# Gate and up of the second layer as seven block products on one Trainium2 core

## The reference, cut to what matters

```python
FF_DIM = 2816
def swiglu(h, w_gu, w_dn):
    g, u = jnp.split(h @ w_gu, 2, axis=-1)
    return (jax.nn.silu(g) * u) @ w_dn
x = post_norm(x, g2 * swiglu(modulate(x, sh2, sc2), w_gate_up[layer], w_down[layer]), ln2_w[layer], ln2_b[layer])
```

## Time and profile before

| what | us |
|---|---|
| median of 3 runs | 1629.88 |
| lowest and highest run | 1629.54, 1630.83 |
| profiled execution, first to last instruction | 1629.1 |
| TensorE busy | 1592.0 |
| VectorE busy | 783.9 |
| ScalarE busy | 427.1 |
| POOL busy | 855.8 |

### The profile page before, as it was taken

How to read it: one execution, slowest core, us unless ns; L and a number is a source line. 1 busy time by engine, 2 the same in 40 slices (tenths; PEclk the granted TensorE clock), 3 DMA queues, 4 the chain that set the end, 5 groups by cost and what they waited for, 6 DMA issues and landing times.

```text
span 1629.1 us, 23301 instructions
## 1 busy us (share of the span) xinstructions
PE 1592.0 (98%) x9335; PEld 1358.5 (83%) x9335; DVE 783.9 (48%) x1201; ACT 427.1 (26%) x920; POOL 855.8 (53%) x850
## 2 busy tenths in 40 slices
PE   7999999999999999999999999999999999999997
PEld 5788666778999988899999888886778888888886
DVE  4352265549663414443555396715659322520038
ACT  5512365425400011100002065216534200200011
POOL 4643044633464444544445455613485777777772
PEclk9999999999999999999999999999999999999999
DMA  9312143121453312244561121210032642233321
GB/s 343 118 52 78 41 149 118 57 78 52 119 165 92 117 40 78 67 146 124 177 210 60 66 78 53 78 52 9 15 85 74 195 142 91 90 95 101 104 91 52
DMA packets 161369, 160.89 MB, mean 99 GB/s; under 512 B 6520, under 2 KB 120296, under 8 KB 161264
## 3 DMA queue, kind: packets, MB, share of 16 engines
q1 hardware_dynamic: 140928, 121.40, 24.5%
q10 hardware_dynamic: 20336, 38.03, 7.2%
HBM read 157.31 MB, written 2.10 MB: 98 GB/s over the span
## 4 chain that ended last, share of the span: by engine, by line
PE 86%; DVE 7%; ACT 4%; issue 2%; DMA 1%; SPq 0%; DVEq 0%; POOL 0%; ACTq 0%
PE ps L843 24%; PE ps L845 24%; PE ps L844 24%; PE ps L1123 3%; PE ps L1147 2%; PE ps L1171 2%; ACT probs L1845 1%; DVE resid L2271 1%; DVE act_lo L2184 1%; DVE st L2212 1%; DVE ps L2193 1%; ACT hbuf L1647 1%; PE ps L966 1%; ACT probs_more L1845 1%; PE ps L927 1%
## 5 line engine op out<-in xcount | busy, mean ns | idle before, releaser
L757 POOL TENSOR_SCALAR ring_hi<-stage 128x512 fp32r<-128x512 f32 x352 | 245.3, 697 | 519.5 <-PE ps L845 450.0
L760 POOL TENSOR_TENSOR ring_lo<-stage,ring_hi 128x512 fp32r<-128x512 f32 x352 | 480.8, 1366 | 29.4
L843 PE MATMUL ps<-act_hi,ring_hi 128*128 128x384 f32 (+2 forms) x1088 | 379.1, 348 | 0.5 <-POOL ring_lo L760 0.5
L845 PE MATMUL ps<-act_hi,ring_lo 128*128 128x384 f32 (+2 forms) x1088 | 377.8, 347 | 0.0
L844 PE MATMUL ps<-act_lo,ring_hi 128*128 128x384 f32 (+2 forms) x1088 | 377.8, 347 | 0.0
L843 PE MATMUL ps<-ring_hi,act_hi 128*128 128x512 f32 (+1 forms) x711 | 280.6, 395 | 0.4 <-DVE act_lo L2184 0.4
L845 PE MATMUL ps<-ring_hi,act_lo 128*128 128x512 f32 (+1 forms) x711 | 273.5, 385 | 0.0
L844 PE MATMUL ps<-ring_lo,act_hi 128*128 128x512 f32 (+1 forms) x711 | 273.1, 384 | 0.0
L843 PEld LDWEIGHTS ps<-act_hi,ring_hi 128*128 128x128 f32 x1088 | 204.6, 188 | 13.9 <-POOL ring_lo L760 0.7
L845 PEld LDWEIGHTS ps<-act_hi,ring_lo 128*128 128x128 f32 x1088 | 204.5, 188 | 13.2
L844 PEld LDWEIGHTS ps<-act_lo,ring_hi 128*128 128x128 f32 x1088 | 204.6, 188 | 13.0
(11 more groups left out here) (278 smaller groups left out, 2046.1 us busy)
## 6 DMA issues: line engine op xcount, KB each, us to landing
stage<-in_w_gate_up_dram SPq DMA_DIRECT2D x88, 512.0 KB, 5.1
mod_stage<-in_w_mod_dram ACTq DMA_DIRECT2D x56, 512.0 KB, 4.2
stage<-in_w_in_dram SPq DMA_DIRECT2D x18, 1024.0 KB, 5.0
stage<-in_w_down_dram SPq DMA_DIRECT2D x16, 1024.0 KB, 5.0
stage<-in_w_mod_dram SPq DMA_DIRECT2D x12, 1024.0 KB, 5.2
start_mod<-in_w_mod_dram SPq DMA_DIRECT2D x16, 512.0 KB, 9.7
stage<-in_w_down_dram SPq DMA_DIRECT2D x8, 768.0 KB, 4.4
stage<-in_w_out_dram SPq DMA_DIRECT2D x16, 256.0 KB, 4.5
```

The lines of the kernel that those rows point to most:

```text
L757: nc.gpsimd.tensor_scalar(hi_, stage[:, par, j * 512:(j + 1) * 512], 1.0, 0.0, ALU.mult, ALU.add).then_inc(w_hi, 1)
L760: nc.gpsimd.tensor_tensor(lo_, stage[:, par, j * 512:(j + 1) * 512], hi_.bitcast(F32), ALU.subtract).then_inc(w_ready, 1)
L843: nc.tensor.matmul(o, a_hi, b_hi, start=first, stop=False)
L845: return nc.tensor.matmul(o, a_lo, b_hi, start=False, stop=last)
```

## The change

The second layer's chunks 3 to 10 of the first half and 0 to 10 of the second half are made by a seven-product scheme for 2 x 2 blocks. The blocks of the weights are gate and up (rows of the result) by the lower and upper 512 of the contraction; those of the activations are the two halves of the contraction by two halves of 256 latent tokens. Each of the seven products is 4 x 3 = 12 matmuls of 256 columns on one slot of 128 x 512.

- SyncE writes the stage as four blocks, `(g k c)` and not `(k g c)`.
- Four of the left operands are blocks of the weights (one of them changed in place by a sum), three are sums of blocks in `w_sum`. VectorE makes the four sums (`fast_sum`), ScalarE the seven high parts (`fast_highs`), POOL five low parts (`fast_low`), VectorE the low parts 3 and 4 (`fast_lows`, `BY_DVE`).
- The right operands that are sums or differences of token blocks are made once: VectorE `t_sums` (seven instructions) at the start of the first half, ScalarE `t_highs` (six), VectorE `t_lows` (six) behind chunk 0's product. For this the four tiles of modulated rows are all kept (`h_rows`).
- TensorE's `fast_chunk` puts products 0 to 3 into four banks' halves, and 4, 5, 6 on top of banks of 0, 1 and 3. ScalarE copies product 0 out (`fast_copy`); VectorE joins in five steps (`fast_half`), waiting for products 2, 3, 5 and 6.
- A chunk takes 7 slots and not 4.

The diff, cut to its core:

```diff
+FIRST_FAST = {(DEPTH - 1, 0): 3, (DEPTH - 1, 1): 0}
+STEPS = 7
+BY_DVE = (3, 4)
...
+        def fast_left(u, i):
+            block = {0: 0, 1: 2, 4: 1, 5: 3}
+            if i in block:
+                return stage[:, u % 2, block[i] * 512:(block[i] + 1) * 512]
+            return w_sum[{3: 0, 2: 1, 6: 2}[i]][:, :]
...
+            def fast_low(l, u, g, i):
+                pool.wait_ge(ring_used, g - 7)
+                pool.wait_ge(sem("fast_hi"), slots_of((ACT_HIGH, DVE_LOW), g))
+                nc.gpsimd.tensor_tensor(ring_lo[:, g % RING, :], fast_left(u, i), ring_hi[:, g % RING, :].bitcast(F32),
+                                        ALU.subtract).then_inc(w_ready, 1)
...
+                def fast_chunk(g, f):
+                    c = fast_number(l, fh, f)
+                    if f >= 2:
+                        need(pe, "hid_ready", l, f0 + f - 1)
+                    elif f == 1:
+                        need(pe, "dn_read", l, 2 * len(tiles_of(l)))
+                    for i, (gu, r) in enumerate(((0, 0), (1, 0), (1, 1), (0, 1), (0, 0), (1, 0), (0, 1))):
+                        slot_wait(pe, g + i)
+                        if c == 0 and i in T_DONE:
+                            need(pe, "t_done", l, T_DONE[i])
+                        if i == 4:
+                            need(pe, "fast_copy", l, c + 1)
+                        elif i > 4:
+                            need(pe, "fast_read", l, 3 * c + i - 3)
+                        b_hi, b_lo = fast_right(i)
+                        for k in range(4):
+                            w = slice(k * P, (k + 1) * P)
+                            mm = joined(fast_bank(l, fh, f, gu, r), ring_hi[:, (g + i) % RING, w], ring_lo[:, (g + i) % RING, w],
+                                        b_hi[:, k, :], b_lo[:, k, :], i < 4 and k == 0, k == 3)
+                        mm.then_inc(ring_used, 1)
...
+            def fast_highs(l, fh, f):
+                g, u = gu_slot(l, fh, f), UNIT0[(l, f"gu{fh}")] + f
+                c = fast_number(l, fh, f)
+                unit_wait(act, u)
+                for i in range(STEPS):
+                    act.wait_ge(ring_used, g + i - 7)
+                    if i in SUM_STEP:
+                        need(act, "fast_sum", l, 4 * c + SUM_STEP[i])
+                    a.activation(ring_hi[:, (g + i) % RING, :], fast_left(u, i), ACT.Copy).then_inc(sem("fast_hi"), 1)
+                    if i == 0 and f and is_fast(l, fh, f - 1):
+                        fast_copy(l, fh, f - 1)
...
+                if (l, fh) == (DEPTH - 1, 0):
+                    t_highs(l)
                 for f in range(HALF):
+                    if f < HALF - 1 and is_fast(l, fh, f + 1):
+                        fast_highs(l, fh, f + 1)
...
                         if fh == 0:
                             act.wait_ge(ffn_mod_used, ffn_units((l, fh)))
                         for j in range(4 if fh else 2):
                             hid_high(l, 2 * fh, j)
-                    chunk(f, g0 + 4 * f + 4, fh * HALF + f - 1 if f >= 2 else None)
+                    chunk(f, gu_slot(l, fh, f) + 4, fh * HALF + f - 1 if f >= 2 else None)
                     load_mods(f)
...
+            def fast_half(l, fh, f, between):
+                g, c = gu_slot(l, fh, f), fast_number(l, fh, f)
+                _, g2, u1, u2 = (fast_bank(l, fh, f, gu, r) for gu in range(2) for r in range(2))
+                more = f < HALF - 1
+                def after(i):
+                    dve.wait_ge(ring_used, g + i + 1)
+                if more:
+                    fast_sum(l, fh, f + 1, 0)
+                    fast_sum(l, fh, f + 1, 1)
+                after(2)
+                need(dve, "fast_copy", l, c + 1)
+                done(v.tensor_tensor(both[:, :], one[:, :], u2, ALU.add), "fast_read")
+                done(v.tensor_tensor(one[:, :], both[:, :], u1, ALU.add), "fast_read")
+                if more:
+                    fast_sum(l, fh, f + 1, 2)
+                after(3)
+                done(v.tensor_tensor(u2, one[:, :], g2, ALU.add), "fast_read")
+                if more:
+                    fast_sum(l, fh, f + 1, 3)
+                    fast_lows(l, fh, f + 1)
+                between()
+                after(5)
+                link(v.tensor_tensor(u1, both[:, :], u1, ALU.add))
+                after(6)
+                done(v.tensor_tensor(g2, both[:, :], g2, ALU.add), "fast_gate")
...
                 for f in range(HALF):
+                    if is_fast(l, fh, f):
+                        fast_half(l, fh, f, first_slices if f == HALF - 1 else lambda: ffn_terms((l, fh), f))
+                        need(dve, "silu_ready", l, fh * HALF + f + 1)
+                        chunk(f)
+                        continue
...
                     chunk(f)
+                    if (l, fh, f) == (DEPTH - 1, 0, 0):
+                        t_lows(l)
                     ffn_terms((l, fh), f)
...
+                if fh == 0 and is_fast(l, 1, 0):
+                    for n in range(4):
+                        fast_sum(l, 1, 0, n)
+                    fast_lows(l, 1, 0)
```

More of the change, by code:

```diff
@@ L69, in plan @@
             slots += max(n, 0)
+            kinds += [DVE_LOW if j in BY_DVE else ACT_HIGH for j in range(n)] if n == STEPS else [POOL_ALL] * max(n, 0)
             mods += n == 0
@@ L73, in plan, with slots_of, gu_slot @@
             units.append((key, n, own if n < 0 else slots, mods, sent[len(units) % 2]))
-    return order, unit0, slot0, units
-ORDER, UNIT0, SLOT0, UNITS = plan()
+    return order, unit0, slot0, units, kinds
+POOL_ALL, ACT_HIGH, DVE_LOW = range(3)
+ORDER, UNIT0, SLOT0, UNITS, SLOT_KINDS = plan()
+def slots_of(kinds, g):
+    return sum(k in kinds for k in SLOT_KINDS[:g + 1])
+def gu_slot(l, fh, f):
+    return SLOT0[(l, f"gu{fh}")] + sum(segment((l, f"gu{fh}"))[:f])
 FFN_MODS = {(0, 0): [(1, "modA", 0), (0, "modC", 0), (1, "modA", 1), (0, "modC", 1)],
@@ L386, in gate_banks @@
         def gate_banks(l, fh, f):
[L388 removed]
+            parts = 2 if is_fast(l, fh, f) else len(token_parts(l))
             if f % 2:
@@ L824, in _ @@
                         g0 -= n
+                    if n == STEPS:
+                        for j in range(STEPS):
+                            if j not in BY_DVE:
+                                fast_low(l, u0, g0 + j, j)
+                        g0 += n
+                        u0 += 1
+                        continue
                     for j in range(n):
@@ L845, in product, with joined @@
                 return nc.tensor.matmul(o, a_lo, b_hi, start=False, stop=last)
+            def joined(o, a_hi, a_lo, b_hi, b_lo, first, last):
+                nc.tensor.matmul(o, a_hi, b_hi, start=first, stop=False, skip_group_check=True)
+                nc.tensor.matmul(o, a_hi, b_lo, start=False, stop=False, skip_group_check=True)
+                return nc.tensor.matmul(o, a_lo, b_hi, start=False, stop=last, skip_group_check=True)
             def keep_clock(bank, n):
@@ new lines, in t_lows, with fast_sum @@
+            def t_lows(l):
+                for n, (i, j) in enumerate(T_ORDER):
+                    need(dve, "t_hi", l, n + 1)
+                    if i == 5:
+                        dve.wait_ge(ring_used, gu_slot(l, 0, 1))
+                    hi_, lo_ = (t_part(x, j) for x in fast_right(i))
+                    done(low(lo_, t_source(i, j), hi_), "t_done")
+            def fast_sum(l, fh, f, n):
+                u, g = UNIT0[(l, f"gu{fh}")] + f, gu_slot(l, fh, f)
+                c = fast_number(l, fh, f)
+                s1, s2, s4 = (w[:, :] for w in w_sum)
+                a11, a12, a21, a22 = (stage[:, u % 2, b * 512:(b + 1) * 512] for b in range(4))
+                if n == 0:
+                    unit_wait(dve, u)
+                before = g - STEPS if f else gu_slot(l, 0, HALF - 1)
+                if c and n != 1:
+                    slot_wait(dve, before + (3, 1, 2, 6)[n])
+                if n == 0:
+                    ins = v.tensor_tensor(s1, a21, a22, ALU.add)
+                elif n == 1:
+                    ins = v.tensor_tensor(a21, a11, a21, ALU.subtract)
+                elif n == 2:
+                    ins = v.tensor_tensor(s2, s1, a11, ALU.subtract)
+                else:
+                    ins = v.tensor_tensor(s4, a12, s2, ALU.subtract)
+                done(ins, "fast_sum")
```

149 lines of the change are left out of this document (121 added, 28 removed).

## The result

The changed kernel takes **1671.16 us** (median of 4 runs, 1671.09 to 1671.2), the kernel before 1630.36 in the runs beside it: a ratio of **1.0251**, 95% interval 1.0236 to 1.0265. The forecast was 1671.5. The profiled execution took 1671.09 with a span (first to last instruction) of 1669.2 us, 40.1 more than the 1629.1 of the earlier trace rows.

A forecast was written before the change was run, and what follows sets the result against it. VectorE was taken to bound the changed kernel through its waits for POOL: 1629.1 + 28.9 (first half) + 12.7 (second half) = 1670.7 us of span, plus 0.8, so 1671.5 us; range 1634 to 1690.

The forecast's parts named there:

- the 0.8 us added for the way from span to device time: Whole kernel: the runs' median, 1629.88, lies 0.8 us above the profiled span, so 1670.7 of span becomes 1671.5.
- Matmuls: Fast chunks: 84 matmuls of 256 columns at 0.120 us take 10.08 us, saving 0.80 a chunk, -15.2 over 19 chunks.
- VectorE's prices: VectorE in a fast chunk: 512-wide SBUF steps 0.69 us, 256-wide joins from PSUM 0.42, undisturbed round 8.1 us.
- Waits at the pair: Fast chunks: POOL's low parts delay VectorE by up to 1.15 us each, 3.9 a round, making the round 12.0.
- Rounds with terms: First half, chunks 3 to 7, where VectorE also adds modulation columns: 14.5 us a round, 0.98 more in chunks 3 and 7.
- Start: First half's start: token sums and pairs make TensorE begin chunk 2 late by 2.1 us; chunk 3's joins reach 1306.9.
- Second half: Second half's gate and up: 131.4 us against 119.7, plus some 1 us of wait in the down projection, +12.7 us.
- Down projection between: Between the halves: highs, sums and two lows put behind the hidden lows cost nothing there; VectorE comes free 7.2 us after the start.
- the bound at TensorE: Rival: sums and lows mostly fall between POOL's steps, the round stays under 10.08 us, total 1619; chance 0.10.
- The rival with the clock: Rival: TensorE, resting 2 of 12 us, is granted 1.2 GHz, a chunk takes 20 us, total 1750; chance 0.03.

The follow-up runs named there:

- first: The changed kernel with POOL's five low parts of each fast chunk cut to 8 of 512 columns, part of the computation left out: 1622.62 us.
- fifth: The changed kernel with the weight sums for products 2 and 3 in PSUM and VectorE making low parts 2 and 3, not 3 and 4: 1639.12 us.
- last run: The kernel with sums in PSUM, start at chunk 8 and later token sums, plus two hidden low parts moved behind the last chunk's silu product: 1622.72 us.
- the run before it: The changed kernel with two weight sums in PSUM, the first half fast from chunk 8 and the tokens' sums behind chunk 3: 1625.26 us.

## Why the prediction was right

The mechanism and the size of the round came out as forecast. That the total is within 0.4 us is luck: the span of 1669.2 is 1.5 us under the forecast 1670.7, and the 0.8 us added for the way from span to device time should have been 1.9 (1671.09 less 1669.2). The 0.8 compared the median of three runs with the span of one; a run of the kernel before has 1.9 too (1630.02 with a span of 1628.1). Term by term:

- *Matmuls*: 0.120 apart at 256 columns, 10.08 a chunk. The rounds that nothing delays show exactly 10.08 (first, fifth and last run).
- *VectorE's prices*: 0.42 for the 256-wide joins with a PSUM operand, a value that no row of the kernel before had; measured 0.42 to 0.43.
- *Waits at the pair*: 3.9 a round expected, 3.9 measured; round 12.0 expected, 12.10 to 12.12 measured. Even the order held: first and third sum long, second and fourth short, both low parts long. By the rule of the Trainium skill (SBUF — State Buffer, "SBUF: two separate sides") that the loser of the pair is fully blocked, the round would have been 12.6; VectorE ended 0.55 after POOL, not 0.69, so the measurement stood.
- *Rounds with terms*: 14.5 expected, 15.5 where an item ends. The second join of chunks 3 to 9 starts 14.74, 14.32, 14.58, 14.59, 15.28 and 12.11 apart, against 15.5, 14.5, 14.5, 14.5, 15.5 and 12.0.
- *Start*: chunk 2 late by 2.1, measured 2.16. The second join of chunk 3 was put at 1306.9; it came at 1304.44 in a trace that runs 1.1 us early there, so 1.4 sooner. The rounds are 0.9 shorter in sum. At TensorE the first half came out at +27.3 and not +28.9.
- *Second half*: +12.7 expected (131.4 us for gate and up, and some 1 us for the last hidden chunk); measured at TensorE 131.97, so +12.3, and 1.4 behind it, of which 1.28 is that rest: +13.7. Two small errors cancel here: the second join came 8.60 us after the start, not 9.55, and nine rounds of 12.11 in place of 12.0 bring both to 117.6.
- *Down projection between*: nothing expected, 0.2 measured. The 1.1 us by which this trace is early ahead of the stage were in no term; nothing was changed there.
- *Rivals*: the bound at TensorE asked for waits under 2.0 a round and promised 1619. Without the waits the kernel took 1622.6, so this rival's mechanism was right, its price within 4 us, and its condition not met. The clock stayed at 0.996 on average; the last section has its falls.

What was missed cost nothing that shows. In chunks 3 to 8 TensorE also rests ahead of product 4, for 0.82 to 3.10 us, until ScalarE has copied product 0. In chunk 3 (3.10 us) that copy is queued behind the transfer of modulation weights, which waits for VectorE's terms. In chunks 4 to 8 it is queued behind the silu of the chunk before, which waits for the last join, and that join stands behind the terms. Timeline of TensorE in the changed kernel, chunks 3 and 8:

```profile
1304.00 0.55 PE L959 MATMUL ps<-act_hi,ring_hi 128*128 128x256 f32 x1 [3.10 <-ACT one L2188]
...
1375.18 0.55 PE L959 MATMUL ps<-act_hi,ring_hi 128*128 128x256 f32 x1 [2.26 <-ACT one L2188]
```

VectorE's first joins of these chunks begin right behind its sums (0.03 to 0.09 us), and it never waits for the products behind them, so its own queue sets the rounds, as worked out. That is read from the trace; no run took this wait away by itself.

## What to carry to other kernels

When work moves to an engine that "has room", add up its queue for one round of the loop, with the meetings on the port pair that it shares with POOL: here 8.1 us of VectorE work became 12.1, and an arithmetic saving of 0.80 us a chunk became a loss of 1.2, and of 3.4 to 4.4 in the chunks with modulation terms. The cure here was to give instructions that meet POOL an operand in PSUM, where banks have unused columns. Then start the scheme where its queue carries nothing else, and look last at the entry and exit chunks, each worth a microsecond or two.

## What the hardware showed beyond this

TensorE's granted clock fell for a few us behind some of its rests, a thing that no slice of the page shows. The windows of the changed kernel around the rest that ends at 1375.18:

```profile
1372.00:1375.00 3.00, 0.91 (x8) 0.71 (x6) 2.20 (x4) 1.36 (x3) 0.07 (x1) 1.00 0.99 276
1375.00:1377.00 2.00, 1.82 (x8) 1.85 (x9) 1.93 (x3) 0.03 (x1) 1.19 (x1) 0.53 0.36 88
1377.00:1379.00 2.00, 1.56 (x10) 1.29 (x9) 1.90 (x4) 0.63 (x1) 0.67 (x1) 0.61 0.00 0
1379.00:1382.00 3.00, 2.41 (x21) 2.24 (x20) 2.75 (x4) 1.74 (x4) 1.59 (x2) 1.00 0.01 3
```

And its matmuls behind that rest:

```profile
1375.53 0.42 PE L960 MATMUL ps<-act_lo,ring_hi 128*128 128x256 f32 x1
1375.74 0.41 PE L961 MATMUL ps<-act_hi,ring_lo 128*128 128x256 f32 x1
1375.96 0.41 PE L959 MATMUL ps<-act_hi,ring_hi 128*128 128x256 f32 x1
```

They are 0.21 apart where they are 0.120 at the full clock: 1.2 and not 2.4 GHz. The rests of 2.16 and 3.10 us in this kernel and that of 1.95 in the run with the joins first were followed by the same (0.63 in the latter's window from 1452 to 1456), those of 1.71 us and less were not. Length alone doesn't settle it: in the run with all low parts on POOL a rest of 2.07 us was followed by 0.52, while rests of 2.09 and 3.09 us were followed by 1.00; and a rest of 1.82 us was followed by 1.00 in the changed kernel (at 1475.91) but by 0.58 in the run with the late start in SBUF (window 1452 to 1456). What decides stays open.

The rival with the clock had TensorE at 1.2 GHz for half of the time; in the changed kernel it fell three times in this stage (the windows of the two halves have 0.96 and 1.00 in the mean), and that cost nothing visible, since VectorE sets the pace. Where TensorE sets the pace it is on the path. In the run from chunk 8 it cost 1.9 us, as above. In the run with the joins first TensorE needed 1.97 us more for the gate and up of the second half than in the run before it (114.53 for 112.56). The longer rest (1.95 for 0.66 + 0.59) accounts for 0.70 of it, and the matmuls at 0.21 behind it, some 16 of them, for an estimated 1.4.
